# A simulated per-engine timing model sets the order in which an encoder kernel's generators emit their instructions

## The reference, cut to what matters

```python
p = einsum('btd,de->bte', x, w_in)                    # 1024 -> 2816
rq, rk, rv, rg, sq, sk, sv = split(p)                 # rope on rq, rk, sq, sk
o, S = retention(rq, rk, rv, S)                       # scores*decay @ v + q @ S; S = decay*S + k^T v
ret = silu(rg) * groupnorm(o) * gn_w
swa = softmax(sq @ sk_window / 8, with a sink) @ sv_window
x = layer_norm(ALPHA*x + concat(ret, swa) @ w_out)    # 1024 -> 1024
h = square(relu(x @ w_up))                            # 1024 -> 4096
y = layer_norm(ALPHA*x + h @ w_down)
```

## Time and profile before

| | us |
|---|---|
| median of 3 runs | 1282.66 (1279.88 to 1338.16) |
| the profiled execution, its own time | 1280.18 |
| its span (slowest core, first to last instruction) | 1277.4 |
| spans of the 8 cores | 1274.7 to 1277.4 |
| phase 1 (until the first up-projection matmul) | about 711 |
| one stage of phase 1, from stage 2 on | about 37.5 |

### The profile page before, as it was taken

The page is one execution under the profiler, slowest core; times in us unless marked ns, Lnnn a source line. Parts: engine busy times, 40 slices in busy tenths (PEclk is TensorE's granted clock), DMA queues, the critical chain, the costliest instruction groups (busy, mean ns, idle before and its releaser), DMA issues.

```text
span 1277.4 us, 15617 instructions; the slowest of 8 cores (1274.7 to 1277.4 us)
## 1 busy us (share of the span) xinstructions
PE 954.9 (75%) x4838; PEld 451.2 (35%) x4838; DVE 546.4 (43%) x1268; ACT 416.8 (33%) x893; POOL 250.6 (20%) x330
## 2 busy tenths in 40 slices
PE   2667667666766766766663699989998999779792
PEld 0133333333333333333321444444444444334341
DVE  0144555555555545555553222211111114772637
ACT  1254444554544455454331322211111111111110
POOL 7300000000000000000013422252234233332320
PEclk9588888889888888888875799999998999889997
DMA  9931011100101110100005930053007100110101
GB/s 183 163 82 34 17 34 34 34 25 27 35 17 34 34 34 18 34 22 1 13 20 81 173 62 1 1 78 56 1 1 105 29 1 5 66 50 17 48 20 66
DMA packets 29586, 55.89 MB, mean 44 GB/s; under 512 B 4034, under 2 KB 13314, under 8 KB 29506
## 3 DMA queue, kind: packets, MB, share of 16 engines
q0 software_dynamic: 18256, 24.81, 13.4%
q1 hardware_dynamic: 11250, 30.10, 7.2%
HBM read 70.23 MB, written 9.47 MB: 62 GB/s over the span
## 4 chain that ended last, share of the span: by engine, by line
PE 57%; DVE 18%; issue 8%; ACT 8%; DMA 4%; POOL 2%; DVEq 1%; ACTq 0%; POOLq 0%; SPq 0%
PE pb L172 57%; DVE yacc L172 5%; DMA WA<-w_in 4%; DVE lst L172 3%; DVE rt L172 3%; DVE on L172 2%; POOL hT L172 1%; ACT Sg L172 1%; ACT rden L172 1%; DVE mix_tm L172 1%; ACT hr L172 1%; DVE scT L172 1%; DVE swaT L172 1%; ACT x1bf L172 1%; ACT xT L172 1%
## 5 line engine op out<-in xcount | busy, mean ns | idle before, releaser
L172 PE MATMUL pb<-WA,xT 128*128 128x512 bf16 (+2 forms) x816 | 231.9, 438 | 13.2 <-DMA WA<-w_in 11.3
L172 PE MATMUL pb<-x1T,WA 128*128 128x512 bf16 (+1 forms) x1120 | 218.0, 345 | 14.2 <-ACT hr L172 13.2
L172 POOL TENSOR_TENSOR hT<-hr 128x512 bf16<-128x512 bf16 (+1 forms) x160 | 156.3, 983 | 350.0 <-ACT hr L172 349.0
L172 DVE TENSOR_TENSOR yacc<-yacc,pb 128x512 f32<-128x512 f32 (+1 forms) x136 | 93.0, 686 | 280.3 <-PE pb L172 279.4
L172 ACT ACTIVATE hr<-pb 128x512 bf16<-128x512 f32 (+1 forms) x160 | 82.9, 522 | 381.3 <-PE pb L172 353.3
L172 PEld LDWEIGHTS pb<-x1T,WA 128*128 128x128 bf16 x1120 | 97.9, 100 | 123.6 <-issue 18.7
L172 PE MATMUL pb<-WA,hT 128*128 128x512 bf16 (+1 forms) x544 | 129.8, 399 | 12.7 <-POOL hT L172 12.3
L172 PEld LDWEIGHTS pb<-WA,xT 128*128 128x128 bf16 (+1 forms) x816 | 89.2, 114 | 138.1 <-issue 97.1
L172 DVE TENSOR_TENSOR rt<-pb,rtab_sb 128x256 f32<-128x256 f32 (+5 forms) x272 | 65.5, 302 | 159.6 <-PE pb L172 136.7
L172 POOL TENSOR_TENSOR gw<-gw,gnw_b 128x512 f32<-128x512 f32 (+1 forms) x17 | 21.5, 1263 | 572.3 <-ACT gw L172 572.3
L172 PE MATMUL pb<-WB,hT 128*128 128x512 bf16 (+1 forms) x544 | 123.5, 385 | 9.1 <-POOL hT L172 9.1
(11 more groups left out here) (114 smaller groups left out, 1048.3 us busy)
## 6 DMA issues: line engine op xcount, KB each, us to landing
rtab_sb<-rtab SPq DMA_DIRECT2D x17, 520.0 KB, 3.7
xf<-xp SPq DMA_DIRECT2D x16, 512.0 KB, 3.2
y_p<-yacc SPq DMA_DIRECT2D x16, 512.0 KB, 2.6
WA<-w_up POOLq DMA_DIRECT2D x28, 256.0 KB, 9.5
WA<-w_in POOLq DMA_DIRECT2D x40, 128.0 KB, 26.9
WA<-w_down POOLq DMA_DIRECT2D x16, 256.0 KB, 15.9
WB<-w_down POOLq DMA_DIRECT2D x16, 256.0 KB, 14.9
WB<-w_out POOLq DMA_DIRECT2D x8, 256.0 KB, 29.6
```

The costliest lines, as they stand in the source:

```text
L172: ins = getattr(eng, o.meth)(*o.args, **o.kw)
```

## The change

Every recorded instruction gets an estimated finish time. `_estimate` keeps one free time for each engine, takes the start as the later of that and of its dependences' finishes (0.25 us added across engines), and adds a duration from a formula: 2400 elements a microsecond for PE, 1200 for ACT plus 0.2, 960 for DVE plus 0.1, 500 for POOL plus 0.2, and 150 KB a microsecond plus 2 for a DMA. `run_scheduled` replaces the turn-taking in phase 1: it always takes a step of that generator whose last step has the earliest estimated finish. And the two attention heads become generators of their own (`swa_group_gen`), so that a stage has four: the chain of front and out_proj_ln1, ret_gen, and one for each head. The set of instructions is the same as before; what differs is their order, and with it the waits.

```diff
+        self._estimate(o, deps)
         return o
+    def _estimate(self, o, deps):
+        try:
+            if o.is_dma:
...
+                issue = 0.7 if o.eng == "pool" else 0.1
+                dur = 2.0 + nbytes / 150e3
+            elif o.eng == "pe":
+                mov = o.kw.get("rhs", o.args[2] if len(o.args) > 2 else None)
+                n = self._free_size(mov) if mov is not None else 128
+                dur = max(0.06, n / 2400.0 + 0.03)
+                issue = dur
+            else:
+                n = self._free_size(o.args[0]) if o.args else 64
+                rate = {"act": 1200.0, "dve": 960.0, "pool": 500.0, "sp": 1000.0}[o.eng]
+                dur = n / rate + (0.2 if o.eng != "dve" else 0.1)
+                issue = dur
...
+        for d in deps:
...
+            f = getattr(d, "fin", 0.0) + (0.25 if (d.eng != o.eng or d.is_dma) else 0.0)
+            if f > ready:
+                ready = f
+        start = max(ready, self.eng_free[o.eng])
+        self.eng_free[o.eng] = start + issue
+        o.fin = start + dur
+        if o.fin > self.step_fin:
+            self.step_fin = o.fin
...
+        def swa_group_gen(t, g):
+            p = t % 2
+            bufs = (5, 6, 0, PT, "PT") if g == 0 else (7, 6, 256, PT2, "PT2")
+            for cc in range(2):
+                for _ in swa_chain(t, p, g, cc, bufs):
+                    yield
...
+        def run_scheduled(gens):
+            live = [[g, 0.0] for g in gens if g is not None]
+            while live:
+                live.sort(key=lambda e: e[1])
+                ent = live[0]
+                P.step_fin = 0.0
+                try:
+                    next(ent[0])
+                    if P.step_fin > 0.0:
+                        ent[1] = P.step_fin
+                except StopIteration:
+                    live.remove(ent)
...
-            bk = back_prompt(t) if t < NTP else back_sample()
-            run_interleaved([a, bk])
+            if t < NTP:
+                run_scheduled([a, ret_gen(t), swa_group_gen(t, 0), swa_group_gen(t, 1)])
+            else:
+                run_scheduled([a, back_sample()])
```

More of the change, by code:

```diff
@@ L26 @@
 class Op:
-    __slots__ = ("eng", "meth", "args", "kw", "deps", "is_dma", "needs_inc", "sem", "val")
+    __slots__ = ("eng", "meth", "args", "kw", "deps", "is_dma", "needs_inc", "sem", "val", "fin")
     def __init__(self, eng, meth, args, kw, is_dma):
@@ L38, in __init__ @@
         self.val = None
+        self.fin = 0.0
 class Res:
@@ L55, in __init__ @@
         self.barrier_op = None
+        self.eng_free = {e: 0.0 for e in ENGS}
+        self.step_fin = 0.0
     def R(self, name):
@@ L93, in op, with _free_size @@
         self.ops.append(o)
+        self._estimate(o, deps)
         return o
+    @staticmethod
+    def _free_size(ap):
+        n = 1
+        for d in ap.shape[1:]:
+            n *= int(d)
+        return n
+    def _estimate(self, o, deps):
+        try:
+            if o.is_dma:
+                ap = o.kw["out"]
+                nbytes = self._free_size(ap) * int(ap.shape[0]) * 4
+                issue = 0.7 if o.eng == "pool" else 0.1
[10 more added lines that the diff above has]
+                issue = dur
+        except Exception:
+            dur, issue = 0.3, 0.3
+        ready = 0.0
+        for d in deps:
+            if d is o:
+                continue
+            f = getattr(d, "fin", 0.0) + (0.25 if (d.eng != o.eng or d.is_dma) else 0.0)
[6 more added lines that the diff above has]
+            self.step_fin = o.fin
     def barrier(self, skip=()):
```

## The result

| | before | after |
|---|---|---|
| median, us | 1281.34 (10 runs) | 1375.71 (9 runs) |
| the profiled execution, us | 1280.18 | 1377.82 |
| its span, us | 1277.4 | 1376.0 |
| first up-projection matmul at | 710.87 | 810.13 |
| from there to the end of the span | 566.5 | 565.9 |

The changed kernel is slower, 1.0741 [1.0729, 1.0752]. All of the loss lies in phase 1. The forecast was 1334 with a range of 1298 to 1360: the direction was right, the size was not, and the time lies outside the range.

A forecast was written before the change was run, and what follows sets the result against it. Phase 1 was taken as a chain from engine to engine, no engine full. Stages growing from 37.20 to 41.45 us gave +55 over thirteen, the others -2; on 1280.2 that is 1333, stated as 1334, range 1298 to 1360.

The forecast's parts named there:

- C: Stretch of a phase 1 stage from the rope of q to the end of mix_tm: 12.1 us predicted, 13.44 before.
- E: New stretch on ACT from v_tm to sq_tm, with both table loads in it: 7.5 us a stage predicted.
- the clock stays up: Rival, chance 0.10: PE's stops are too short for its clock to fall; stage 37.4 us, time about 1281.
- mix_tm is in time: Rival, chance 0.05: PE does not wait at the mix_tm transposes; stage 33.95 us, time 1236, faster.
- the order doesn't change what matters: Rival: the same engine still ends the stage; about 1281, counted within the clock rival's case, no chance of its own.
- Drains: Rival, chance 0.05: ACT stands still about 1.28 us behind each table load; time 1367.
- G: Output projection on PE, at a lower clock after PE's standing: 4.9 us predicted, bounds 3.6 and 5.0; 3.62 before.
- B: From the first matmul of proj(0) to q's rope, clock rising within proj(0): 2.8 us predicted, 3.50 before.
- D: From the end of mix_tm to the projection copy v_tm, at half clock: 3.8 us predicted, 3.76 before.
- F: From sq_tm to the output projection, same rope, transposes and copies: 3.5 us predicted, 3.48 before.
- S, gst, gmv and swaT are done before q's rope: Claimed DVE order in stages 0 and 1, shortening the way to mix_tm; +1.9 us each, +4 together.

## Why the prediction was wrong in size

**The mechanism held.** DVE's order ahead of mix_tm, C, was 11.97 us for 12.1. ACT's stretch, E, was 7.77 for 7.5, with both loads in it, without a hole, and PE in wait. Taking the loads out gave 59 us in the new order and nothing in the old. The lines by group, over the whole kernel:

```profile
L215 PE MATMUL pb<-ident_sb,sq_tm 128*64 128x128 bf16 (+1 forms) x136 | 12.7, 248 | 53.1 <-DVE rt L215 46.6 <-DVE sq_tm L215 6.5
...
L215 PE MATMUL pb<-ident_sb,mix_tm 128*128 128x128 bf16 (+1 forms) x68 | 9.7, 296 | 85.9 <-DVE mix_tm L215 85.9
```

The stop for mix_tm does not go, as the prediction had it: 4.2 to 4.9 us in stages 2 to 14, where it was 4.67. That its sum, 85.9 us, is to the tenth what it was before is chance, since in stages 0 and 1 it grew from under 5 to over 8. The stop for the rope of sq_tm is new: 53.1 us where that group had 6.2. The rivals: "the clock stays up" is refuted by the windows, "mix_tm is in time" by the stops of 4.2 us and more, and "the order doesn't change what matters" by the same stop at sq_tm. Drains: not there.

**The step that failed is the price of the half clock behind a stop, in G first, and in B and D.** G said "five at 0.216 are 1.1", that is, the half clock would cost the output projection the time of five matmuls. The window it rests on (688.6 to 695.9 and the 3 us behind the earlier trace rows) was a stretch in which PE had been busy half the time, and the clock was back at 1.00 from about 699 on, behind nine matmuls. Here PE had stood for 3.31 us, and twelve matmuls took 5.00 us at 0.50, the clock rising only in the last four. G was 6.38 in this stage and 5.57 in the mean of the thirteen, not 4.9, and outside its bound of 5.0. B said "the clock should rise within proj(0)" and took 2.8; the mean is 3.47, hardly less than the 3.50 it was taken from. D took "at the same half clock" and before's 3.76 with it, a stretch whose window was at 0.57; 343.3 to 347 was at 0.50 throughout, and D was 4.18. These three are 0.67 + 0.67 + 0.38 = 1.7 of the 2.46 us by which the mean stage, 43.91, is longer than the 41.45 worked out. E gives another 0.5 and F 0.4. That part is not the clock alone: the rope of sq_tm starts 0.85 us after sq_tm in place of 0.69, behind a swaT multiply, and E is 9.95 us in one stage. Filling the stops takes 82 us away without starting mix_tm any earlier, which is what says that this is the clock and not another wait. Which difference between the two stretches made the clock rise later here is not shown.

**Stages 0 and 1 failed by reading.** The step was "S, gst, gmv and swaT are done before q's rope", for +1.9 each. DVE's timeline in stage 0:

```profile
74.06 1.54 DVE L215 TENSOR_TENSOR rt<-pb,rtab_sb 128x256 f32<-128x256 f32 x4 [4.75 <-PE pb L215]
...
76.39 1.46 DVE L215 SCALAR_TENSOR_TENSOR S<-S,pb 128x128 f32<-128x128 f32 x4
...
84.65 0.69 DVE L215 TENSOR_TENSOR mix_tm<-on,gw 128x512 bf16<-128x512 f32 x1 [0.17 <-DVE on L215]
```

S, gst and gmv (79.36) stand behind q's rope, so their 4.0 us are on the way to mix_tm there too, and PE's row is

```profile
85.49 0.58 PE L215 MATMUL pb<-ident_sb,mix_tm 128*128 128x128 bf16 x4 [8.49 <-DVE mix_tm L215]
```

a stop of 8.49 us. v_tm to sq_tm was 8.63 (89.58 to 98.21), as predicted (8.4). The two stages and what leads up to them lose 18.1 us instead of 4; S, gst and gmv are 8 of the 14 us between, and the retention matmuls, which now stand ahead of proj(0) and had been given no time there, are some 2.5. Against the profiled execution the sum was 45 us short (98.6 for 53): 27 in the thirteen stages (2.46 each, less the 0.37 by which the stage that was cut up, 37.20, was shorter than the mean before, 37.57), 14 here, 2 in stage 15, and 2 at the end of phase 1 (-5.1 for -6.8).

**The range.** Its bounds added each piece's own bound, and those of G and D were too narrow for a clock that differs from stage to stage. And no bound was made for a wrongly read order.

## What to carry to other kernels

Look at what an order made by a model leaves out of its prices: here the duration formulas knew neither ACT's table loads nor that PE slows down behind a stop, and the order put both loads on the chain and cut PE's standing time into four pieces. Look at what lies inside each engine's stop before moving work out of it; table loads that cost nothing there cost 59 us once they were outside, about half of it by their own length and most of the rest by the clock behind the stop they made. Where a kernel is a chain between engines, price a stop of TensorE as the stop plus the half clock of what follows, by the windows behind the nearest stop of that length, and look at several stages, since one stage is no measure of it: G was 4.4 in one and 6.4 in another.

## What the runs showed of the hardware that I had not expected

- The clock row still read 1.00 through a standstill of 3.3 us, 0.64 in the 1.7 us of small transposes behind it, and 0.50 through the 5 us of full work that followed.
- The penalty is not in proportion to the stop. In one kernel the same small stops (0.29 and 1.14 us) had the clock at 1.00 behind them in one stage and at 0.79 in another, and stages of 34.2 and 37.5 us came in the same run.
- Matmuls whose results nobody reads were worth 36 us in one place and 82 in four, 6% of the kernel, with everything else unchanged. In the kernel before, holding the clock across two stops made it fall in the output projection, where it had never been low.
